# Scan gate and norm moved between the steps of the output product; the scan's state part scaled in its PSUM bank

## The chip, the cores and the metric

The kernel runs on 1 core of one Trainium2 chip. The metric is the device time of one execution in microseconds (us). Names of engines as in the profile: PE is TensorE (PEld its weight loads), DVE is VectorE, ACT is ScalarE, POOL is GpSimd, SP is the engine that issues most DMAs (SPq is its queue of instructions). Loops count from 0.

## The reference

The program is two layers of one hybrid block (attention, convolution, recurrence, Fourier mix), and then one layer of a second block: latent attention, a state-space scan over 10 chunks of 128 positions with 16 heads in both directions, a gate, a norm, an output product, and a feed-forward part. The change lies in the second block alone:

```python
# y: the scan's output (1024 positions x 1024), both directions and the skip term added up
# z: a gate, silu(projection), computed earlier and stored in HBM
y = y * z
y = y * rsqrt(mean(y * y, axis=-1) + EPS) * ssd_norm_2
mix = concatenate([attention (1024 columns), y (1024 columns)], axis=-1) @ w_out_2   # 2048 x 1024
x = x + gate * rms_norm(mix, mix_post_norm_2)
```

In the scan, the output of a chunk has a state part, `(C S) * exp(a)` (S is the state carried from chunk to chunk, `exp(a)` one factor for each position and head), and a part within the chunk. Everything is float32.

## The kernel before, in words

Each stage is a block with one instruction list per engine and a barrier at its end (`k.done`); nothing of a stage starts before all engines have left the one before. The order within a stage is written out by hand, and semaphores pass results between engines. The three stages in question:

**The scan, `ssd_scan` (L1825).** Ten units u; w is the direction (0 forward, 1 backward), g a group of 8 heads (512 columns). The first two units carry only the state; units 2 to 9 (i = u - 2 is 0 to 7) give output. POOL multiplies the inputs by the factors of their positions (`weigh`, L1908: xw for the state, xd for the part within the chunk), decays the state (`decay`, L1926, L1936) and writes the skip term `xs * skip` as the first value of y (`skip_terms`, L1902, L1904). PE does the state part (`off`, L1954), the state's increment (`inc`, L1961) and, per unit, eight products within the chunk (`diag`, L1997). DVE multiplies the state part by `exp(a)` out of PSUM into an SBUF tile `tmp` (L2041) and adds `tmp` to y (`add`, L2053, both operands in SBUF), adds the increment to the state (`state`, L2061), masks the exponentials (`mask`, L2072), and adds the part within the chunk from PSUM to y (`diag`, also L2053). Three PSUM banks are shared in turn by `off` and `inc`: `wait_bank` (L1882) makes a product wait for the one three turns earlier to be used.

**The gate and norm, `normalize` (L579, called at L3738).** For each of 8 tiles of 128 positions: DVE multiplies y by z (L704), ACT squares and sums (L729), DVE and ACT form the root and its reciprocal (L672, L732, L676), DVE scales (L718), PE transposes 8 blocks (L774), ACT and DVE move four of them each into `ssd_t`, multiplied by the gain (L739, L684). SP loads the z tiles (L802), the 4 MB of attention output (L805) and, after the last z, the first three weight chunks (L126).

**The output product, `project_normalize` (L2550, called at L3742).** Tiles in groups of 3, 3 and 2; each group takes 16 steps kk over 2048 rows of weights: kk 0 to 7 read the attention output, kk 8 to 15 `ssd_t`. In a step ACT rounds the input and one row block of weights (L2869, L2873), DVE forms what the rounding left (L2773, L2776), and PE does 3 products for each tile and half (L2903 to L2905). Rounded tiles are two or three deep, so ACT runs up to two steps ahead of PE. At kk 1 to 7 of groups 1 and 2 the same engines also do the residual, norm and transposes of the group before (`norms`). Before its second step DVE combines some rows that POOL and SP have loaded (`constants`, L2684). Weights come in chunks of 2 MB for 4 steps, in a ring of 3.

The weights' ring lies where the scan keeps its tiles, so the first chunk can't be loaded before the scan is over.

## Time and profile before

| | before |
|---|---|
| median of 3 runs | 4858.21 us (4854.99 to 4859.52) |
| the profiled execution | 4853.79 us, its span 4851.9 us |
| PE, DVE, ACT, POOL busy | 85%, 58%, 44%, 21% of the span |
| the scan, 3563 to 3779 us | 216 us, granted PE clock 0.90 |
| gate and norm, 3779 to 3834 us | 55 us, granted PE clock 0.50 |
| output product, 3834 to 4057 us | 223 us, granted PE clock 0.94 |

Rows of the timeline have the start in the span, the time from the first start to the last end of the instructions merged in them, engine, line, operation, tiles, and how many. In brackets stands how long the engine was idle before, and what ended that. The granted clock is a share of the full one: 0.50 is the lower of its two levels (1.2 GHz), 1.00 the upper (2.4 GHz).

### The profile page before, as it was taken

What the parts mean: (1) busy time and instruction counts of PE and PEld (TensorE: products, weight loads), DVE (VectorE), ACT (ScalarE), POOL (GpSimd) and SP (SyncE); (2) the same over time, 40 slices, a digit from 0 to 9 for tenths busy, and PEclk for the clock granted to TensorE, in tenths of its full rate; (3) what the DMA queues carried; (4) which work ended last, traced back from release to release, by engine and by line L of the source; (5) the groups of instructions that cost most, each with busy time, mean ns of one, the idle gap of its engine ahead of it and who ended that gap; (6) DMA issues with size and microseconds to landing.
All of it is one profiled execution on the core that took longest, in us unless ns stands there. A gap on an engine that the chain in (4) does not pass through costs nothing. (4 is left out here: it accounts for less than half of the span.)

```text
span 4851.9 us, 58640 instructions
## 1 busy us (share of the span) xinstructions
PE 4126.1 (85%) x21892; PEld 3166.3 (65%) x21892; DVE 2830.4 (58%) x4301; ACT 2151.2 (44%) x3807; POOL 1011.2 (21%) x1178
## 2 busy tenths in 40 slices
PE   5989798977989887976779999979949687999898
PEld 4765576766765666655547667657736576888676
DVE  3745566966655557965434544535967555565545
ACT  4532245424532346324446666644524344444334
POOL 0001002510001001500047777720046000110100
PEclk7989899988999998988989999989969798999999
DMA  5100012554100011032000000022000434111233
GB/s 161 35 14 1 32 44 97 211 183 161 38 18 1 32 35 61 2 99 86 19 12 8 5 5 5 1 87 62 10 2 1 178 130 118 35 53 52 74 139 135
DMA packets 178077, 295.81 MB, mean 61 GB/s; under 512 B 43322, under 2 KB 105914, under 8 KB 177796
## 3 DMA queue, kind: packets, MB, share of 16 engines
q1 hardware_dynamic: 177044, 291.83, 17.8%
q8 instruction: 177, 2.90, 0.3%
q14 instruction: 104, 0.85, 0.1%
q0 software_dynamic: 608, 0.08, 0.0%
q10 hardware_dynamic: 144, 0.15, 0.0%
HBM read 261.53 MB, written 30.51 MB: 60 GB/s over the span
## 5 line engine op out<-in xcount | busy, mean ns | idle before, releaser
L497 DVE TENSOR_TENSOR x_low<-buf_a,x_high 128x1280 fp32r<-128x1280 f32 (+5 forms) x368 | 373.8, 1016 | 441.4 <-ACT x_high L466 438.3
L523 PE MATMUL ps<-x_high,w_high 128*128 128x512 f32 (+1 forms) x1344 | 497.4, 370 | 106.1 <-DVE w_low L501 101.5
L466 ACT CAST x_high<-buf_a 128x1280 fp32r<-128x1280 f32 (+5 forms) x368 | 324.8, 882 | 570.5 <-PE ps L525 490.5
L524 PE MATMUL ps<-x_low,w_high 128*128 128x512 f32 (+1 forms) x1344 | 485.4, 361 | 0.0
L525 PE MATMUL ps<-x_high,w_low 128*128 128x512 f32 (+1 forms) x1344 | 484.4, 360 | 0.0
L2903 PE MATMUL ps<-w_high,x_high 128*128 128x512 f32 x896 | 369.4, 412 | 109.7 <-DVE w_low L2776 64.6
L3185 POOL TENSOR_TENSOR probs_low<-kr_t,probs_high 128x512 fp32r<-128x512 f32 x320 | 411.2, 1285 | 181.4 <-ACT probs_high L3318 123.1
L3342 DVE TENSOR_REDUCE mx<-ps 128x1 f32<-128x1280 f32 x128 | 191.0, 1492 | 327.8 <-PE ps L3213 327.2
L523 PEld LDWEIGHTS ps<-x_high,w_high 128*128 128x128 f32 x1344 | 259.7, 193 | 178.1 <-DVE x_low L497 116.9
L2904 PE MATMUL ps<-w_low,x_high 128*128 128x512 f32 x896 | 362.6, 405 | 0.0
L2905 PE MATMUL ps<-w_high,x_low 128*128 128x512 f32 x896 | 361.5, 404 | 0.0
L2776 DVE TENSOR_TENSOR w_low<-w,w_high 128x1024 fp32r<-128x1024 f32 x170 | 208.2, 1224 | 256.9 <-ACT w_high L2873 256.8
L2873 ACT CAST w_high<-w 128x1024 fp32r<-128x1024 f32 x170 | 178.2, 1049 | 339.4 <-PE ps L2905 339.4
L2204 PE MATMUL ps<-x_high,w_high 128*128 128x512 f32 x704 | 278.4, 395 | 13.0 <-DVE w_low L2300 13.0
L525 PEld LDWEIGHTS ps<-x_high,w_low 128*128 128x128 f32 x1344 | 259.1, 193 | 38.5
L2903 PEld LDWEIGHTS ps<-w_high,x_high 128*128 128x128 f32 x896 | 177.0, 197 | 161.9 <-issue 124.6
L524 PEld LDWEIGHTS ps<-x_low,w_high 128*128 128x128 f32 x1344 | 260.0, 193 | 32.6
L2206 PE MATMUL ps<-x_high,w_low 128*128 128x512 f32 x704 | 279.8, 397 | 0.0
L2205 PE MATMUL ps<-x_low,w_high 128*128 128x512 f32 x704 | 278.9, 396 | 0.0
L523 PE MATMUL ps<-w_high,x_high 128*128 128x512 f32 (+2 forms) x608 | 219.0, 360 | 61.0 <-DVE w_low L501 57.4
L2296 DVE TENSOR_TENSOR x_low<-attn_t,x_high 128x512 fp32r<-128x512 f32 x176 | 145.6, 828 | 203.6 <-ACT x_high L2249 193.4
L3314 ACT ACTIVATE kr_t<-ps 128x512 f32<-128x512 f32 x320 | 191.6, 599 | 135.2 <-PE ps L3244 74.8
(418 smaller groups left out, 9512.0 us busy)
## 6 DMA issues: line engine op xcount, KB each, us to landing
w<-in_w_out SPq DMA_DIRECT2D x26, 2048.0 KB, 8.2
w<-in_w_mod SPq DMA_DIRECT2D x24, 2048.0 KB, 9.0
w<-in_w_down SPq DMA_DIRECT2D x15, 2048.0 KB, 8.2
w<-in_w_in SPq DMA_DIRECT2D x26, 1024.0 KB, 5.5
w<-in_w_up SPq DMA_DIRECT2D x22, 1024.0 KB, 7.6
w<-in_w_in SPq DMA_DIRECT2D x7, 2048.0 KB, 8.7
x<-in_x SPq DMA_DIRECT2D x16, 512.0 KB, 4.5
scratch_x<-x SPq DMA_DIRECT2D x16, 512.0 KB, 5.2
```

The lines of the kernel that those rows point to most:

```text
L466: act.copy(xh[i % NX][:, 0:s["tn"]], x_of(s)).then_inc(x_high, 1)
L497: dve.tensor_tensor(xl[i % NX][:, 0:s["tn"]], x_of(s), xh[i % NX][:, 0:s["tn"]].bitcast(F32), ALU.subtract).then_inc(x_low, 1)
L523: pe.matmul(g["out"], lhs[0][:, :], rhs[0][:, :], start=(s["kk"] == 0), stop=False)
L524: pe.matmul(g["out"], lhs[0][:, :], rhs[1][:, :], start=False, stop=False)
L525: mm = pe.matmul(g["out"], lhs[1][:, :], rhs[0][:, :], start=False, stop=s["last"])
L2204: pe.matmul(o, wh[w % NW][:, c], xh[x % NX][:, :], start=(kk == 0), stop=False)
L2205: pe.matmul(o, wh[w % NW][:, c], xl[x % NX][:, :], start=False, stop=False)
L2206: mm = pe.matmul(o, wl[w % NW][:, c], xh[x % NX][:, :], start=False, stop=(kk == KD - 1))
L2903: pe.matmul(o, a[:, t], wh[i % NW][:, c], start=(s["kk"] == 0), stop=False)
L2904: pe.matmul(o, a[:, t], wl[i % NW][:, c], start=False, stop=False)
L2905: mm = pe.matmul(o, b[:, t], wh[i % NW][:, c], start=False, stop=s["last"])
L3185: pool.tensor_tensor(prl[g % NPR][:, :], pt[g % NPT], prh[g % NPR][:, :].bitcast(F32), ALU.subtract).then_inc(probs_low, 1)
```

## The change

**In the scan.** `off` on DVE writes its product back into the PSUM bank it read, and `add` takes it from there; `tmp` is gone. The bank is therefore free only after the addition: `wait_bank` waits for `off_added`. POOL issues the skip terms of two chunks after `decay(u)` and ahead of `weigh(u + 1)`, for u = 1 to 4; before it was after `weigh(u + 1)`, for u = 0 to 3.

**Between scan and product.** The `normalize` call is gone. A class `StateNorm` gives ACT, DVE and PE lists of work by step of the product, and `project_normalize` issues one item of each after every step. Tiles 0 to 2 are done in steps 0 to 7 of group 0, tiles 3 to 5 in its steps 8 to 15, tiles 6 and 7 in steps 8 and following of group 1. y is gated and scaled in place; afterwards its rows hold the product's own scratch tiles. The z tiles have three buffers, so the load of tile n, from n = 3 on, waits on SP until tile n - 3 is squared. Each list yields once per step. The attention output comes in three pieces, by group.

```diff
@@ wait_bank
-                pe.wait_ge(off_used, nth(u - CT_, w, g) + 1)
+                pe.wait_ge(off_added, off_at[u, w, g])
@@ POOL
                 decay(u)
+                if 1 <= u < 5:
+                    skip_terms(u - 1)
+                    skip_terms(NLT - u)
                 if u + 1 < U:
                     weigh(u + 1)
-                if u < 4:
-                    skip_terms(u)
-                    skip_terms(NLT - 1 - u)
@@ DVE, off
-                b = tmp[g]
+                o = ps[:, bank_of("off", u, w, g), :]
                 dve.wait_ge(off_ready, nth(i, w, g) + 1)
-                dve.tensor_tensor(heads(b[:, :]), heads(ps[:, bank_of("off", u, w, g), :]), per_head(eac, CT_ + t, g, w), ALU.mult
-                                  ).then_inc(off_used, 1)
-                dve.wait_ge(off_used, nth(i, w, g) + 1)
-                add(t, g, b[:, :])
+                dve.tensor_tensor(heads(o), heads(o), per_head(eac, CT_ + t, g, w), ALU.mult).then_inc(off_scaled, 1)
+                dve.wait_ge(off_scaled, nth(i, w, g) + 1)
+                add(t, g, o)
@@ new class
+class StateNorm(Beside):
+    WINDOWS = {0: (0, 1, 2), KD: (3, 4, 5), 3 * KD: (6, 7)}
+    GATE, SQUARE, MEAN, SCALE, TURN, OUT = (0, 0, 1), (1, 1, 2), (2, 2, 3), (3, 3, 4), (3, 4, 5), (5, 6, 7)
...
+    def load(self, sp, weights):
...
+        attn(0)
+        weights(1)
+        for n in range(3):
+            z(n)
+        sp.dma_start(self.gcol[:, :], self.gain.rearrange("(k p) -> p k", p=P)).then_inc(self.gain_in, 16)
+        weights(3)
+        attn(1)
+        attn(2)
+        for n in range(3, 8):
+            z(n)
...
+    def dve(self, dve):
...
+            for n in ga:
+                dve.wait_ge(self.z_in[n % 3], 16 * (n // 3 + 1))
+                dve.tensor_tensor(self.y[:, n, :], self.y[:, n, :], self.z[n % 3][:, :], ALU.mult).then_inc(self.gated, 1)
...
+    def pe(self, pe, banks_free):
+        for tu in self.parts(self.TURN):
+            for n in tu:
+                banks_free(pe)
+                if n >= 1:
+                    self.wait_banks(pe)
+                pe.wait_ge(self.scaled, n + 1)
...
@@ project_normalize, DVE (ACT and PE alike)
+            parts = beside.dve(dve) if beside else iter(())
             for i, s in enumerate(steps):
...
                 norms(s["kk"], before[s["g"]])
+                next(parts, None)
@@ project_normalize, SP
+            if beside:
+                beside.load(sp, lambda m: ws.load_until(sp, first_chunk + m - W_SLOTS))
+                ws.load_until(sp, first_chunk + 3)
             def load(n):
+                if beside and n < NS:
+                    sp.wait_ge(beside.transposed, 2 * (NS + n + 1))
@@ second_block
-    normalize(k, [dict(t=t, stream=0, src=d["z"][(t - CT_) * P:(t - CT_ + 1) * P, :], res=True, yt=t - CT_, store=None)
-                  for t in range(CT_, NT)], ssdT, None, d["ssd_norm_2"][0], lay, y=y, gates=None,
-              moves=[(attnT[:, :, :], d["attn"].rearrange("(c p) t -> p c t", p=P))])
...
+                      post=d["mix_post_norm_2"][0], beside=StateNorm(k, y, ssdT, d["ssd_norm_2"][0], attnT, rooms))
```

The order on POOL at the scan's start, where xw, xd are weighed inputs, s the states and ssd_y the skip terms. Before:

```order
L1914 TENSOR_TENSOR xw_453_34884<-xs_32719,w_end_34751 128x512 x2
L1914 TENSOR_TENSOR xw_455_34886<-xs_32719,w_end_34751 128x512 x2
L1904 TENSOR_TENSOR ssd_y_34882<-xs_32719,skip_34750 128x512 x4
L1936 TENSOR_TENSOR s_456_34887<-s_457_34888,tot_34752 128x512 x2
L1936 TENSOR_TENSOR s_458_34889<-s_459_34890,tot_34752 128x512 x2
L1914 TENSOR_TENSOR xw_452_34883<-xs_32719,w_end_34751 128x512 x2
L1914 TENSOR_TENSOR xw_454_34885<-xs_32719,w_end_34751 128x512 x2
```

and in the changed kernel, at the same place:

```order
L1915 TENSOR_TENSOR xw_453_34884<-xs_32719,w_end_34751 128x512 x2
L1915 TENSOR_TENSOR xw_455_34886<-xs_32719,w_end_34751 128x512 x2
L1937 TENSOR_TENSOR s_456_34887<-s_457_34888,tot_34752 128x512 x2
L1937 TENSOR_TENSOR s_458_34889<-s_459_34890,tot_34752 128x512 x2
L1905 TENSOR_TENSOR ssd_y_34882<-xs_32719,skip_34750 128x512 x4
L1915 TENSOR_TENSOR xw_452_34883<-xs_32719,w_end_34751 128x512 x2
L1915 TENSOR_TENSOR xw_454_34885<-xs_32719,w_end_34751 128x512 x2
```

The decay of unit 1 now comes ahead of the first skip terms; the input of unit 2 keeps its place.

The order of DMA issues on SP after the scan, before:

```order
L802 DMA x_479_36777<-scratch_z 128x1024
L802 DMA x_480_36778<-scratch_z 128x1024
L802 DMA x_481_36779<-scratch_z 128x1024
L805 DMA attn_t_22019<-scratch_attn 128x8x1024
```

and in the changed kernel (xn is the place of the row that `constants` reads):

```order
L3071 DMA gate_row_497_36793<-scratch_mod 128x1024
L3074 DMA xn_494_36790<-in_mix_post_norm 128x1024
L2583 DMA attn_t_22019<-scratch_attn 128x8x384
L126 DMA w_3_51<-in_w_out 128x4x1024
L2580 DMA z_477_36775<-scratch_z 128x1024
L2580 DMA z_478_36776<-scratch_z 128x1024
L2580 DMA z_479_36777<-scratch_z 128x1024
L2589 DMA gain_col_36778<-in_ssd_norm 128x8x1
L126 DMA w_4_52<-in_w_out 128x4x1024
L126 DMA w_2_50<-in_w_out 128x4x1024
```

Two broadcast rows and a piece of the attention output now stand ahead of the first weight chunk, and the z tiles behind it.

## Rows read from the trace of the kernel before

**Rows 1.** Windows of scan and norm: us, busy by engine, PEclk, DMA share, GB/s.

```profile
3563.00:3779.00 216.00, 165.50 (x816) 117.38 (x816) 151.70 (x188) 74.84 (x160) 135.04 (x128) 0.90 0.00 1
3779.00:3834.00 55.00, 15.93 (x65) 12.76 (x66) 30.41 (x70) 26.42 (x62) 3.55 (x4) 0.50 0.74 277
```

**Rows 2.** Timeline of DVE, first outputs of the scan.

```profile
3583.42 0.69 DVE L2061 TENSOR_TENSOR s<-ps,s 128x512 f32<-128x512 f32 x1 [0.31 <-POOL s L1936]
3586.28 0.69 DVE L2041 TENSOR_TENSOR tmp<-ps,eac 128x512 f32<-128x512 f32 x1 [2.16 <-PE ps L1954]
3587.00 24.87 DVE L2053 TENSOR_TENSOR ssd_y<-tmp,ssd_y 128x512 f32<-128x512 f32 x1
```

**Rows 3.** Timeline of POOL, the same stretch.

```profile
3579.28 4.04 POOL L1936 TENSOR_TENSOR s<-s,tot 128x512 f32<-128x512 f32 x4
...
3607.28 4.04 POOL L1904 TENSOR_TENSOR ssd_y<-xs,skip 128x512 f32<-128x512 f32 x4
3617.96 1.04 POOL L1936 TENSOR_TENSOR s<-s,tot 128x512 f32<-128x512 f32 x1 [6.64 <-DVE s L2061]
```

**Rows 4.** Timeline of PE, first products within the chunk of i = 0 and 1.

```profile
3612.52 1.97 PE L1997 MATMUL ps<-xd,e 128*128 128x64 f32 x8 [25.42 <-DVE e L2072]
...
3636.36 1.10 PE L1997 MATMUL ps<-xd,e 128*128 128x64 f32 x8 [1.96 <-DVE e L2072]
```

**Rows 5.** Timeline of DVE, first items of later units of the scan.

```profile
3633.58 0.69 DVE L2041 TENSOR_TENSOR tmp<-ps,eac 128x512 f32<-128x512 f32 x1 [2.54 <-PE ps L1954]
3634.30 1.40 DVE L2053 TENSOR_TENSOR ssd_y<-tmp,ssd_y 128x512 f32<-128x512 f32 x1
...
3654.41 0.69 DVE L2041 TENSOR_TENSOR tmp<-ps,eac 128x512 f32<-128x512 f32 x1 [2.54 <-PE ps L1954]
...
3760.90 0.69 DVE L2053 TENSOR_TENSOR ssd_y<-tmp,ssd_y 128x512 f32<-128x512 f32 x1
```

**Rows 6.** Timeline from the scan's end to the product's start.

```profile
3778.35 0.69 DVE L2053 TENSOR_TENSOR ssd_y<-ps,ssd_y 128x512 f32<-128x512 f32 x1 [0.60 <-PE ps L1997]
3780.06 1.28 SPq L802 DMA_DIRECT2D x<-scratch_z  x3
...
3797.26 1.22 DVE L704 TENSOR_TENSOR x<-ssd_y,x 128x1024 f32<-128x1024 f32 x1
...
3802.36 1.22 DVE L704 TENSOR_TENSOR x<-ssd_y,x 128x1024 f32<-128x1024 f32 x1
...
3831.38 1.04 ACT L2873 CAST w_high<-w 128x1024 fp32r<-128x1024 f32 x1
...
3833.82 0.77 PE L2903 MATMUL ps<-w_high,x_high 128*128 128x512 f32 x1 [5.13 <-DVE w_low L2776]
```

**Rows 7.** Windows of 4 us: attention load, then broadcasts with x tiles.

```profile
3788.00:3792.00 4.00, 0.00 (x0) 0.00 (x0) 1.39 (x4) 2.63 (x4) 0.00 (x0) 0.50 1.02 416
...
3836.00:3840.00 4.00, 4.00 (x16) 3.21 (x15) 0.00 (x0) 0.12 (x1) 0.00 (x0) 0.84 1.03 243
```

**Rows 8.** DMA issues by line, 3775 to 3850, then 3846 to 4070.

```profile
w<-in_w_out SPq DMA_DIRECT2D x3, 2048.0 KB, 13.2
...
w<-in_w_out SPq DMA_DIRECT2D x9, 2048.0 KB, 7.9
```

**Rows 9.** Timeline of the product: step length on DVE; transposes on PE; start of group 2.

```profile
3959.87 1.23 DVE L2776 TENSOR_TENSOR w_low<-w,w_high 128x1024 fp32r<-128x1024 f32 x1 [2.38 <-ACT w_high L2873]
...
3963.95 1.23 DVE L2776 TENSOR_TENSOR w_low<-w,w_high 128x1024 fp32r<-128x1024 f32 x1 [2.38 <-ACT w_high L2873]
...
3932.20 1.03 PE L2887 MATMUL ps<-ident,xn 128*128 128x128 f32 x8
3932.99 0.48 PE L2903 MATMUL ps<-w_high,x_high 128*128 128x512 f32 x1
...
3844.65 0.47 PE L2903 MATMUL ps<-w_high,x_high 128*128 128x512 f32 x1 [0.79 <-DVE w_low L2776]
...
3985.41 0.77 PE L2903 MATMUL ps<-w_high,x_high 128*128 128x512 f32 x1 [6.32 <-DVE tmp L2702]
```

More of the change, by code:

```diff
@@ L1886, in wait_bank @@
             if kind == "off":
-                pe.wait_ge(off_used, nth(u - CT_, w, g) + 1)
+                pe.wait_ge(off_added, off_at[u, w, g])
             else:
                 pe.wait_ge(state_out, nth(u, w, g) + 1)
+    off_at = {(u, w, g): nth(u - CT_, w, g) + 1 for u in range(CT_, U) for w in range(2) for g in range(2)}
     def diag_bank(g):
@@ L2555, in project_normalize @@
+def project_normalize(k, y, kt, tiles, sizes, xt, mod_cols, gain, lay, gates, post=None, pre=None, stored=None, beside=None):
     nc, ps, d, ws = k.nc, k.ps, k.d, k.ws
@@ L2587, in project_normalize @@
     wh, wl = ([lay(f"w_{p}{i}", [P, D], F32R) for i in range(NW)] for p in ("high", "low"))
-    xs = [lay(f"x{i}", [P, D]) for i in range(NS)]
-    tmp = [lay(f"tmp{i}", [P, D]) for i in range(NB)]
+    places = beside.places if beside else {}
+    xs = places["x"] if beside else [lay(f"x{i}", [P, D]) for i in range(NS)]
+    tmp = places["tmp"] if beside else [lay(f"tmp{i}", [P, D]) for i in range(NB)]
     xn = [lay(f"xn{i}", [P, D]) for i in range(2)] if xt is not None else []
-    trash = lay("trash", [P, D])
+    trash = places["trash"] if beside else lay("trash", [P, D])
     stat = lay("stat", [P, 3, 3, nt])
@@ L2594, in project_normalize @@
     gate_row = {s: lay(f"gate_row{s}", [P, D]) for s in sorted({w["stream"] for w in with_y})}
-    post_row = lay("post_row", [P, D]) if post is not None else None
+    post_row = (xn[0] if beside else lay("post_row", [P, D])) if post is not None else None
     pre_row = lay("pre_row", [P, D]) if pre is not None else None
@@ L2598, in project_normalize @@
     gcol = lay("gain_col", [P, KD])
+    first_chunk = ws.taken - len(groups) * n_chunks
     sems = k.sems("rows_in", "cols_in", "squared", "rooted", "dve_chain", "scaled", "transposed", "evac_act", "evac_dve",
@@ L2794, in square_root @@
                     act.wait_ge(squared, sq_index[n, kind] - 1)
+                elif beside:
+                    act.wait_ge(beside.squared, 6)
                 act.activation(trash[:, :], data, ACT.Square, accum_out=st[:, 0:1]).then_inc(squared, 1)
@@ L2864, in norms @@
                     tile_of(transposes_out, mine, 2)
+            parts = beside.act(act) if beside else iter(())
             for i, s in enumerate(steps):
@@ L2868, in _ @@
                     act.wait_ge(ws.products, steps[i - NX]["after"])
+                if beside:
+                    beside.ready(act, s["g"], s["kk"])
                 act.copy(xh[i % NX][:, 0:s["tn"]], y(s["kk"], s["t0"], s["tn"])).then_inc(x_high, 1)
@@ L2874, in _ @@
                 norms(s["kk"], before[s["g"]])
+                next(parts, None)
             for kk in range(1, 8):
@@ L2879, in _, with banks_free @@
         def _(pe):
+            turned = [0]
+            def banks_free(engine):
+                if turned[0]:
+                    engine.wait_ge(evac_act, turned[0])
+                    engine.wait_ge(evac_dve, turned[0])
+            parts = beside.pe(pe, banks_free) if beside else iter(())
             def transposes(n):
                 pe.wait_ge(scaled, n + 1)
+                turned[0] = n + 1
+                if beside:
+                    beside.wait_banks(pe)
                 for half in range(2):
@@ L2911, in _ @@
                     tile_of(transposes, before[s["g"]], turn_at.index(s["kk"]))
+                next(parts, None)
             if xt is not None:
@@ L2950, in _ @@
                     sp.wait_ge(stored[i], 16 * n_store[i])
-    k.done(sems)
+    k.done(sems + (beside.sems if beside else []))
 class Gates(Beside):
```

102 lines of the change are left out of this document (92 added, 10 removed).

## The prediction

> **What bounds the kernel now.** I read the page first for the whole, then the windows over the second block, then the timelines of one engine after another around each place that the change touches. The whole is PE's: 85% busy. The change lies in three neighbouring stages, and each has another limit.
>
> In the scan PE sets the pace once it runs. A unit takes 20.83 us, from one state part on DVE to the next (3633.58 to 3654.41) [rows 5]. The first unit with output is the exception. DVE's first addition of `tmp` to y starts at 3587.00 and is on record for 24.87 us, where the same operation takes 0.69 us later on [rows 2, 5]. It ends at 3611.87. POOL ran without a gap until 3607.28 + 4.04 = 3611.32 and then waited for DVE [rows 3]. PE stood for 25.42 us, waiting for the mask behind that addition [rows 4]. So one addition held up the three engines. I take the cause to be its two SBUF inputs: the state addition at 3583.42, with one input in PSUM, took 0.69 us while POOL was inside its run of decays that began at 3579.28 [rows 2, 3]. In later units the first such addition takes 1.40 us, and with POOL done with its work, at 3760.90, 0.69 us [rows 5].
>
> The Trainium skill says the same in "SBUF — State Buffer", section "Who interferes with whom": a DVE instruction with two SBUF inputs contends with a GpSimd instruction that reads SBUF, and the pair of ports is an exclusive lock for one whole instruction. By that rule the addition would wait for one POOL instruction, some 1 us; the trace has 24.87 us, so here back-to-back POOL instructions kept it out. By the page alone the change would win about 1 us at this place instead of the 23.1 us below.
>
> Between scan and product PE has 64 transposes in 55 us at a granted clock of 0.50 [rows 1]. The scan's last addition ends at 3779.04, the product's first matmul starts at 3833.82: 54.8 us [rows 6]. Each tile takes 5.10 us there, a chain over DVE, ACT, DVE and PE (3797.26 to 3802.36) [rows 6].
>
> In the product PE sets the pace: a step of three tiles is 4.08 us, and DVE sits idle 2.38 us of it ahead of its weights' part, waiting for ACT, which waits for PE [rows 9].
>
> **The change, part by part.** All sums are against the profiled execution (4853.79 us, its span 4851.9 us). It lies 4.4 us below the median of the runs, so I add the difference to the median at the end.
>
> *1. The long addition.* Its second input is in PSUM now, so it shows no wait for POOL: 0.69 us as at 3583.42. What comes late next is POOL's own work. POOL took 1.01 us for each instruction, four in 4.04 us. The decay of unit 1 started at 3579.28 behind four skip terms [rows 3]; now it starts where those did, at about 3575.3, and is done at 3579.3, and the skip terms of chunks 0 and 7 are done by 3583.3. Unit 2's xw keeps 3583.28 to 3587.28, and the first two xd, which PE's first product within the chunk needs, are done at 3589.28 (two more instructions). DVE's state part, scaling, addition and masks start 4 us earlier than before and are ready by about 3585, so POOL is the last. Before, that product started at 3612.52 [rows 4]; now at 3589.4. Gain 23.1 us. The rest of unit i = 0 I leave as it was: 3636.36 - 3612.52 = 23.84 us [rows 4], 3 us longer than 20.83, from a slow start after PE's idle time. PE will be idle again ahead of it, for about 6 us. POOL's further instructions (decay, skip, xw, xd, 16 of them, 16.2 us) fit into a unit.
>
> *2. The addition in units 1 to 6.* The masks stand behind it on DVE, and PE waits 1.96 us for them [rows 4]. 1.40 becomes 0.69 us, six times: gain 6 x 0.71 = 4.3 us. The later part of a unit is PE's own.
>
> *3. The banks.* The wait for the addition instead of the scaling holds a bank 0.7 us longer. The product three turns on comes at least 2 us later in PE's order: nothing. DVE writing PSUM instead of SBUF isn't in the trace; the nearest rows, reading PSUM, have 0.69 against 0.69 us [rows 2, 5]. I take 0; if it were 0.1 us more for each of 32, with a quarter of them ahead of PE, 1 us.
>
> *4. From the scan's end to the first product.* The first DMA still goes out at 3780.06, 1.0 us after the scan [rows 6]. Ahead of the first weights in the queue stand two broadcast rows (1.0 MB written), 1.6 MB of attention output, then 2.1 MB of weights. Loads of this queue land in its order: three chunks issued at one time landed at 13.2 us in the median, one alone at 7.9 us [rows 8], so a second chunk costs 5.3 us. Large loads ran at 416 GB/s (0.416 MB in a us), the stretch with broadcasts at 243 GB/s [rows 7]. Broadcasts 1.05 / 0.243 = 4.3 us, attention 1.57 / 0.416 = 3.8 us, or, its pieces being 1.5 KB, up to 4.8 us; I take 4.3. A chunk then lands 7.9 us later, its latency in it. Sum: 3780.9 + 4.3 + 4.3 + 7.9 = 3797.4. From the rounding of the weights to the first matmul it is 3833.82 - 3831.38 = 2.4 us [rows 6]. First matmul at 3799.8: 20.8 us after the scan, where it was 54.8. Gain 34.0 us. With all at 416 GB/s it would be 36; with the attention piece and the weights at 243 GB/s too, 28.
>
> *5. The first steps.* PE loses 0.79 us before its third step, because DVE waits for rows that POOL loads [rows 9]. These loads now have the 20 us before the first matmul. Gain 0.8 us.
>
> *6. What the norm costs inside the product.* PE gets 64 transposes: 8 x 0.8 us at the full clock (3932.20 to 3932.99) [rows 9], and perhaps 0.2 us of wait behind each eight. Cost 8 x 0.9 = 7.2 us. DVE's heaviest step has two gates (2 x 1.22 us [rows 6]) beside its own 1.8 us: 4.2 us against 4.08, with a lead of up to two steps, so hidden. ACT's has two squares, below that. Each transpose set waits for the banks of the one before to be emptied, one step later on DVE and ACT; they get to it about 3.7 us after PE has begun the step, and PE needs 5 us for step and transposes: hidden, with about 1 us to spare.
>
> *7. The fourth chunk.* On SP it stands behind the z loads, the last of which waits for the square of tile 4 in step 9. That happens when PE ends step 7, about 3837; with two squares it is 3840.5. Behind the two z tiles (2 x 1.3 us) the chunk lands at about 3840.5 + 1 + 2.6 + 7.9 = 3852; the rounding for step 12 should start by 3852.5. Near the edge: I take 0.5 us, and up to 5 if the queue is slower.
>
> Sum: -23.1 - 4.3 - 34.0 - 0.8 + 7.2 + 0.5 = -54.5 us. On the profiled execution 4799.3; on the median 4803.7. The changes of group (6.32 us of PE idle [rows 9]) and the last group's norm stay.
>
> **The rivals.**
> *A. The long wait moves.* If what holds DVE is not the second SBUF input but any addition into y while POOL runs without a gap, parts 1 and 2 go. For: the state additions that ran beside POOL wrote another tile. Against: the additions of 0.69 us from PSUM to y, and the 24.87 us ends with POOL's run and nothing else. 4858.2 - 27.1 = 4831.
> *B. The queue.* The fourth chunk, a z tile or the first weights come late, 5 us at one, or twice: 3 loads more between others than before. For: SP is one instruction list, and a wait in it holds every later load. Against: rates of [rows 7]. 4809 to 4816.
> *C. More is won.* Without the slow start of unit 0 (3 us) and with the first weights at the better rate (2 us): 4798.
> *D. The other side.* The norm's chain doesn't hide: PE reaches each set of transposes before `scaled` and waits the chain of 5.10 us [rows 6] for each of 8 tiles, 40.8 us, and the clock falls to 0.50 after such waits, as where the product restarted after 6.32 us [rows 9]; with 2 us for each of 8 restarts that is 56.8 us. It turns the result from about 54 us on: 4804 + 57 = 4861. Against: gate, square, mean and scale are each issued one step before they are needed, 4 us for at most 2.5 us of work.
> *E. The change does nothing for the gap*, because the attention output and weights set its length anyway: 5.7 MB and latency. Against: three quarters of that load is now behind the first matmul. It would leave -27 + 7 = -20: 4838.
>
> **How the numbers follow.** The forecast, 4796 to 4810, has 0.62; B 0.15; C 0.12; A 0.06; E 0.02; D 0.02; 0.01 for no difference. What this kernel's measurement can tell from none is 0.2%, 10 us, either way. A, B, C, E and the forecast all lie below 4848: faster 0.97, same 0.01, slower 0.02. The range takes in B and C and their bounds: 4791 to 4820.
>
> **What would show it.** In the scan: no addition into y above 1 us, PE's first product within the chunk near 3589, units of 20.1 us, the scan ending near 3752. Then 20 us, not 55, to the first matmul, which waits for weights, with the lower clock at its start. In the product: 8 transpose sets of about 0.8 to 1 us each, DVE without a wait for POOL's rows, and PE's idle time in step 12 near zero. The prediction is wrong if an addition of PSUM and y waits for POOL, if the first matmul comes later than 28 us after the scan, or if PE waits at the transposes for `scaled`.

## The result, and the profile after

| | before | after |
|---|---|---|
| median of 4 runs each, us | 4857.15 (4854.99 to 4859.52) | 4801.23 (4798.93 to 4803.31) |
| ratio, with its 95% interval | | 0.9885 (0.9868 to 0.9902) |
| profiled execution, us; its span | 4853.79; 4851.9 | 4798.93; 4797.1 |

The change takes 55.9 us off, 1.15%. The forecast was 4803.7 us with a range of 4791 to 4820. In the profiled executions the difference is 54.9 us, where the sum of the terms said 54.5. It comes from these stages, each read between the same two instructions of the two traces:

| stage | from, to | before | after |
|---|---|---|---|
| scan | POOL's first `xw`, end of DVE's last addition into y | 215.99 | 186.71 |
| gap | to the product's first matmul | 54.78 | 20.55 |
| product | to PE's first transposes behind its last wait for DVE | 215.37 | 224.38 |
| tail | to the next stage's first matmul | 19.25 | 19.31 |
| the rest | to the end of the span | 783.46 | 783.53 |

The work ahead of the scan took 0.4 us less by chance (POOL's first `xw` at 3563.05 and at 3562.62); in the kernels below that item starts anywhere from 3560.0 to 3566.0. So single traces are compared by their stages here, not by the time of day in them.

Windows of the scan and of the gap after the change, which answer to [rows 1]; the columns are the same (us, busy time of PE, PEld, DVE, ACT and POOL, PEclk, DMA share, GB/s):

```profile
3562.60:3749.33 186.73, 161.81 (x816) 114.62 (x816) 120.96 (x188) 74.84 (x160) 129.13 (x128) 0.95 0.00 1
3749.33:3769.87 20.54, 0.00 (x0) 0.03 (x1) 1.93 (x4) 2.91 (x4) 2.69 (x3) 0.55 0.90 300
```

DVE's busy time in the scan falls from 151.70 to 120.96 us with the same 188 instructions: most of what went was never work, but waiting that is on record as busy (the long addition alone is 24.2 of these 30.7 us). The mean granted clock rises from 0.90 to 0.95.

DVE's first outputs, against [rows 2], and its first items of two later units, against [rows 5]:

```profile
3580.21 0.70 DVE L2042 TENSOR_TENSOR ps<-ps,eac 128x512 f32<-128x512 f32 x1 [0.51 <-PE ps L1955]
3580.95 0.69 DVE L2053 TENSOR_TENSOR ssd_y<-ps,ssd_y 128x512 f32<-128x512 f32 x1
...
3609.67 0.70 DVE L2042 TENSOR_TENSOR ps<-ps,eac 128x512 f32<-128x512 f32 x1 [2.54 <-PE ps L1955]
3610.40 0.69 DVE L2053 TENSOR_TENSOR ssd_y<-ps,ssd_y 128x512 f32<-128x512 f32 x1
...
3629.79 0.70 DVE L2042 TENSOR_TENSOR ps<-ps,eac 128x512 f32<-128x512 f32 x1 [2.55 <-PE ps L1955]
```

The addition of 24.87 us takes 0.69 us now, and so does each later one. Scaling in the PSUM bank takes 0.70 us where writing `tmp` took 0.69. A unit takes 20.12 us (3609.67 to 3629.79).

PE's first products within the chunk, against [rows 4]:

```profile
3589.06 1.94 PE L1998 MATMUL ps<-xd,e 128*128 128x64 f32 x8 [8.03 <-POOL xd L1924]
...
3611.74 1.10 PE L1998 MATMUL ps<-xd,e 128*128 128x64 f32 x8 [1.25 <-DVE e L2072]
```

In the first, PE waits for POOL's `xd` and no longer for DVE's mask; in the second the wait behind DVE's addition is 1.25 us instead of 1.96.

The gap, against [rows 6] and [rows 8]: the queue and ACT, then the loads between 3749 and 3775 with the median time from issue to landing.

```profile
3750.35 0.33 SPq L3071 DMA_DIRECT2D gate_row<-scratch_mod  x1
3750.73 0.43 SPq L3074 DMA_DIRECT2D xn<-in_mix_post_norm  x1
3751.20 0.43 SPq L2583 DMA_DIRECT2D attn_t<-scratch_attn  x1
3751.68 0.58 SPq L126 DMA_DIRECT2D w<-in_w_out  x1
```

```profile
3762.31 0.51 ACT L3008 CAST x_high<-attn_t 128x384 fp32r<-128x384 f32 x1 [15.58 <-DMA attn_t<-scratch_attn]
...
3767.43 1.04 ACT L3012 CAST w_high<-w 128x1024 fp32r<-128x1024 f32 x1 [4.61 <-DMA w<-in_w_out]
```

```profile
gate_row<-scratch_mod SPq DMA_DIRECT2D x1, 512.0 KB, 4.6
xn<-in_mix_post_norm SPq DMA_DIRECT2D x1, 512.0 KB, 5.6
```

The two rows have landed at about 3755.0 and 3756.3, the attention piece by 3762.3, the first weights by 3767.4, each behind the one before. The product's first matmul follows at 3769.88, 2.45 us after its weights are there.

The product, against [rows 9]:

```profile
3789.13 1.03 PE L2673 MATMUL ps<-ident,ssd_y 128*128 128x128 f32 x8
3789.92 0.48 PE L3055 MATMUL ps<-w_high,x_high 128*128 128x512 f32 x1
...
3794.21 1.03 PE L2673 MATMUL ps<-ident,ssd_y 128*128 128x128 f32 x8
```

A set of eight transposes holds PE for 0.79 us (3789.13 to 3789.92), and none of the eight sets shows a wait for `scaled` or for a bank.

### The profile page after: what moved, and what is told of

It reads as the page before. It is cut to its first block and busy times, and to the rows that moved or that the text cites. A ratio compares the mean times of both kernels' runs of the same rounds, so it can differ in the third digit from the quotient of the medians.

```text
span 4797.1 us, 58620 instructions
## 1 busy us (share of the span) xinstructions
PE 4119.3 (86%) x21892; PEld 3159.2 (66%) x21892; DVE 2796.7 (58%) x4299; ACT 2147.5 (45%) x3807; POOL 1006.1 (21%) x1177
## 3 DMA queue, kind: packets, MB, share of 16 engines
q1 hardware_dynamic: 180164, 291.84, 18.1%
```

## The experiments

Twelve kernels were run. Their medians stand against runs of the kernel before on the same chip. "Scan", "gap" and "product" are the stages of the table above, read from each kernel's own trace.

| kernel | median | against before | ratio (95%) | scan | gap | product |
|---|---|---|---|---|---|---|
| e_psum | 4824.48 | -30.7 | 0.9940 (0.9925 to 0.9954) | 185.79 | 55.39 | |
| e_order | 4851.56 | -3.6 | 0.9993 (0.9983 to 1.0002) | 212.15 | 54.81 | |
| e_norm | 4827.20 | -28.0 | 0.9945 (0.9930 to 0.9960) | 216.06 | 20.68 | 223.52 |
| e_pause | 4832.26 | -22.9 | 0.9954 (0.9940 to 0.9969) | 195.32 | 55.06 | |
| e_early | 4835.47 | -20.0 | 0.9957 (0.9942 to 0.9972) | 195.99 | 54.60 | |
| e_first | 4833.08 | -22.4 | 0.9956 (0.9941 to 0.9971) | 195.43 | 54.76 | |
| e_rows | 4800.45 | -54.5 | 0.9886 (0.9872 to 0.9901) | 186.60 | 17.23 | 224.20 |
| e_xd | 4796.69 | -58.3 | 0.9880 (0.9865 to 0.9894) | 182.49 | 20.52 | 224.61 |
| e_align | 4797.27 | -57.7 | 0.9883 (0.9866 to 0.9899) | 186.58 | 20.55 | 222.10 |
| e_turn16 | 4808.37 | -46.6 | 0.9902 (0.9887 to 0.9917) | 186.53 | 20.53 | 231.72 |
| e_best | 4792.45 | -63.0 | 0.9871 (0.9855 to 0.9888) | 183.45 | 17.71 | 221.08 |
| e_best2 | 4790.30 | -65.2 | 0.9869 (0.9853 to 0.9886) | 184.12 | 17.27 | 220.91 |

### The parts one by one: e_psum, e_order, e_norm

e_psum is the kernel before with the state part scaled in its bank:

```
-                b = tmp[g]
+                o = ps[:, bank_of("off", u, w, g), :]
...
-                dve.tensor_tensor(heads(b[:, :]), heads(ps[:, bank_of(...), :]), per_head(...), ALU.mult)
+                dve.tensor_tensor(heads(o), heads(o), per_head(...), ALU.mult)
...
-                add(t, g, b[:, :])
+                add(t, g, o)
... in wait_bank:
-                pe.wait_ge(off_used, nth(u - CT_, w, g) + 1)
+                pe.wait_ge(off_added, off_at[u, w, g])
```

Expected: 

> The kernel before, with the state part scaled in its PSUM bank and nothing else; POOL keeps its old order and the norm stays a stage of its own. My theory (the second SBUF input lets POOL's back-to-back instructions keep DVE out): the first addition into y takes 0.7 us instead of 24.87, PE's first product within the chunk starts at about 3589 to 3590, later units take 20.1 us: 26 to 28 us less than before, about 4830. Rival A (any addition into y waits for POOL): no change, the long addition stays. A second rival, that the reordering of POOL is needed for the gain: less than 20 us.

Measured: 30.7 us less than before; the scan 30.2 us shorter, where 26 to 28 were expected (the rest is the unit behind the first product, 21.77 us for 23.84, and the slow unit of point 2 below). DVE's and PE's timelines:

```profile
3586.00 0.69 DVE L2054 TENSOR_TENSOR ssd_y<-ps,ssd_y 128x512 f32<-128x512 f32 x1
```

```profile
3588.58 1.07 PE L1999 MATMUL ps<-xd,e 128*128 128x64 f32 x8 [2.50 <-POOL xd L1925]
3610.35 1.11 PE L1999 MATMUL ps<-xd,e 128*128 128x64 f32 x8 [1.25 <-DVE e L2073]
```

POOL, in its old order, had no gap here either (from 3562.16 on), and DVE's addition took 0.69 us inside that run. So the operand in PSUM alone removes the long wait, and rival A falls. The new order of POOL isn't needed; with the operand in PSUM the scan is 0.9 us longer with it (186.71 against 185.79, from one profile of each). PE's product starts 26.42 us after POOL's first item here and 26.44 after the change. But DVE's scaling, addition and masks come later in the old order, so PE stands idle for 2.50 us instead of 8.03 ahead of that product, and the product itself takes 1.07 us instead of 1.94.

e_order moves POOL's skip terms and changes nothing else:

```
                 decay(u)
+                if 1 <= u < 5:
+                    skip_terms(u - 1)
+                    skip_terms(NLT - u)
                 if u + 1 < U:
                     weigh(u + 1)
-                if u < 4:
-                    skip_terms(u)
-                    skip_terms(NLT - 1 - u)
```

Expected: 

> The kernel before, with POOL's skip terms moved ahead of the next unit's weighing and nothing else; the addition keeps tmp in SBUF. My theory: the addition starts some 4 us earlier and still waits until POOL's run ends, which now comes about 4 us earlier because the skip terms of chunks 2 and 5 are behind the decay that waits: an addition of 24 to 26 us, PE's first product within the chunk at about 3608, later units still 20.8 us; 4 to 5 us less than before, about 4853. Rival (the order of POOL is what ended the long wait): 23 us less.

Measured: 3.6 us less, within this measurement's noise; the scan 3.8 us shorter. The addition in DVE's timeline:

```profile
3584.30 26.53 DVE L2053 TENSOR_TENSOR ssd_y<-tmp,ssd_y 128x512 f32<-128x512 f32 x1
```

It is still there, ends at 3610.83, and POOL's run ended at 3610.28 (its last four `xd` are 3606.24 + 4.04). Before the change it ended 0.55 us behind POOL too (3611.87 and 3611.32 [rows 2, 3]). The order of POOL's work alone doesn't end the wait, so the rival falls.

e_norm has the scan of before, with `tmp` and the old order of POOL, and the norm between the steps of the product:

```
-    normalize(k, [...], ssdT, None, d["ssd_norm_2"][0], lay, y=y, gates=None, moves=[...])
-    project_normalize(..., post=d["mix_post_norm_2"][0])
+    project_normalize(..., post=d["mix_post_norm_2"][0],
+                      beside=StateNorm(k, y, ssdT, d["ssd_norm_2"][0], attnT, rooms))
```

Expected: 

> The scan as before (tmp in SBUF, old order of POOL), the norm tile by tile between the steps of the product as in the changed kernel. My theory: the parts add up. The gap from scan to product falls from 54.8 to 20.6 us, the product takes 9 us longer, as in the changed kernel: 25 us less than before, about 4832. Rival (the gap's gain hangs on the faster scan, or the product's loss does): off by more than 5 us from that.

Measured: 28.0 us less by the medians. Counted from POOL's first item, the profiled execution is 23.8 us shorter: scan +0.1, gap -34.1, product +8.2, and 2.1 us more than in the kernel before in what comes behind the product, which the edit doesn't touch. The theory's 25 lies between the two figures. The gap and the product repeat those of the changed kernel within 1 us, so the parts add up. e_psum's scan and this gap make 64.3 us, and with the product's 9 to pay about 55.

### What kept DVE waiting: e_pause, e_early, e_first

These three are the kernel before with one wait added on POOL, each in another place; `tmp` stays in SBUF.

```
e_pause, in the unit loop of POOL:
+                if u == 1:
+                    pool.wait_ge(off_added, 1)
                 if u < 4:
                     skip_terms(u)
e_early, in weigh(u):
+                if u == 2:
+                    pool.wait_ge(off_ready, 1)
e_first, in the unit loop of POOL:
+                if u == 0:
+                    pool.wait_ge(inc_ready, nth(1, 1, 0) + 1)
                 if u < 4:
                     skip_terms(u)
```

Expected of e_pause: 

> The kernel before, with one wait on POOL: after the first unit's xd and before the skip terms of chunks 1 and 6 it waits until the first addition into y is done. My theory (back-to-back POOL instructions keep the addition out, and it gets in when POOL stops): the addition starts near 3587.0 and ends within 1 us of POOL's stop near 3591.3, so 4 to 5 us long instead of 24.87; PE's first product within the chunk near 3593, 18 to 20 us less than before, about 4838. Rival (the addition waits for something else than POOL's run, its tile y or a semaphore): it stays near 25 us and the time doesn't change, or grows by the 4 us that POOL lost.

Measured: 22.9 us less. DVE and POOL:

```profile
3585.20 5.02 DVE L2055 TENSOR_TENSOR ssd_y<-tmp,ssd_y 128x512 f32<-128x512 f32 x1
...
3592.06 0.84 DVE L2055 TENSOR_TENSOR ssd_y<-tmp,ssd_y 128x512 f32<-128x512 f32 x1
```

```profile
3585.64 4.04 POOL L1923 TENSOR_TENSOR xd<-xs,dt 128x512 f32<-128x512 f32 x4
3590.31 4.49 POOL L1904 TENSOR_TENSOR ssd_y<-xs,skip 128x512 f32<-128x512 f32 x4 [0.63 <-DVE ssd_y L2055]
```

POOL stops at 3589.68, the addition ends at 3590.22: once more 0.54 us behind. So it was POOL's run that held it; its tile and its semaphores were ready all along. But the next rows speak against my wording of the cause. From 3590.31 POOL runs without a gap for over 50 us. The additions that meet this run, early or late in it, wait at most 0.8 us (0.84 us long at 3592.06, 1.45 at most), while the first four POOL instructions take 4.49 us instead of 4.04. So it isn't the length of the run either. "POOL back to back keeps DVE out" is too wide: it is true here only of the first run. The next two kernels ask what differs in it.

Expected of e_early: 

> The kernel before, with one wait on POOL in another place: ahead of the first unit's xw it waits until PE has made the first state part, so POOL idles from 3583.3 to about 3586.2 and then runs without a gap again. DVE's first addition into y starts some 0.8 us into that run, not within the idle time. What is open: in the kernel with a pause inside the long addition, later additions that met a gapless run of POOL waited at most 0.4 us, each to about the end of one POOL instruction, while the first one was held for the whole run. Theory 1 (a run of POOL that has once been interrupted lets DVE in at the next instruction's end): the addition takes at most 1.7 us, PE's first product within the chunk near 3592, 18 to 21 us less than before. Theory 2 (DVE's first addition of two SBUF inputs is held until POOL stops, whatever POOL did before): it lasts until the run ends near 3614, the time grows by about 3 us over before.

Measured: 20.0 us less. DVE and POOL:

```profile
3587.48 0.91 DVE L2055 TENSOR_TENSOR ssd_y<-tmp,ssd_y 128x512 f32<-128x512 f32 x1
```

```profile
3586.80 5.01 POOL L1916 TENSOR_TENSOR xw<-xs,w_end 128x512 f32<-128x512 f32 x4 [2.79 <-PE ps L1956]
3591.78 4.04 POOL L1925 TENSOR_TENSOR xd<-xs,dt 128x512 f32<-128x512 f32 x4
```

Expected of e_first: 

> The kernel before, with one wait on POOL still earlier: ahead of its first skip terms (3575.3) it waits for PE's next to last state product of unit 1, an idle time of under 1 us; then it runs without a gap, and DVE's first addition into y meets it some 11 us into that run. With the idle time 3.3 us ahead of the addition (the run before this one) the addition took 0.91 us. Theory 1 (one interruption of POOL since the start of the stage is enough): the addition takes at most 1.7 us, 19 to 22 us less than before. Theory 2 (only a recent interruption lets DVE in; a long run shuts it out again): the addition lasts until the run ends near 3612, the time is within 1 us of before.

Measured: 22.4 us less. DVE and POOL:

```profile
3588.12 1.07 DVE L2055 TENSOR_TENSOR ssd_y<-tmp,ssd_y 128x512 f32<-128x512 f32 x1
```

```profile
3575.60 4.04 POOL L1904 TENSOR_TENSOR ssd_y<-xs,skip 128x512 f32<-128x512 f32 x4 [1.26 <-PE ps L1963]
3579.60 4.04 POOL L1936 TENSOR_TENSOR s<-s,tot 128x512 f32<-128x512 f32 x4
3583.60 4.04 POOL L1914 TENSOR_TENSOR xw<-xs,w_end 128x512 f32<-128x512 f32 x4
3587.60 5.01 POOL L1923 TENSOR_TENSOR xd<-xs,dt 128x512 f32<-128x512 f32 x4
```

Theory 1 holds in both. One idle time of POOL of 1.26 us, 12.5 us ahead of the addition, with no DVE instruction of two SBUF inputs in between, takes the wait from 24 us to 0.4. POOL's group gets longer instead, 5.01 for 4.04 us. The kinds of POOL's instructions are the same in all four kernels, and its run was gap-free at the addition in each. What differs is only whether POOL has paused since it began the stage. A wait that is met at once isn't enough: in the kernel before, POOL's decays and `xw` between 3595 and 3603 wait for semaphores and lose no time by it, and the addition stays held. Nor does the idle time ahead of the stage count, 365 us in the kernel before. Why a run that never paused since then holds DVE to its end isn't settled by these runs, and all of them look at one place of one kernel.

### The sizes of the other terms: e_rows, e_xd, e_align, e_turn16

All four are the changed kernel with one edit.

```
e_rows, in StateNorm.load (the two broadcasts are a function now, called here and not first):
         attn(0)
         weights(1)
         for n in range(3):
             z(n)
+        rows()
...
```

Expected: 

> The changed kernel, with the loads of the two broadcast rows (gate and post norm) issued behind the first attention piece, the first chunk of weights and the first three z tiles instead of ahead of them all. My theory for the gap's length (the loads of this queue land in its order, and what stands ahead of the first weights sets the first matmul): the first weights land about 4.3 us earlier, the first matmul comes 16 to 17 us after the scan's end instead of 20.55, and the rows, needed by DVE after step 1, come early enough: 4 us less than the changed kernel, 57 to 61 us less than before. Rival (the weights' own transfer and latency set it, the rows are small): gap within 1 us of 20.55. A second rival: DVE waits for the rows or z between steps 1 and 2, and PE gets the 4 us back as idle time in step 2.

Measured: the gap is 17.23 us, 3.3 less, and nothing is given back in the product (224.20 against 224.38). ACT and DVE:

```profile
3765.66 1.04 ACT L3013 CAST w_high<-w 128x1024 fp32r<-128x1024 f32 x1 [4.73 <-DMA w<-in_w_out]
```

```profile
3772.64 1.23 DVE L2826 TENSOR_TENSOR gate_row<-gate_row,xn 128x1024 f32<-128x1024 f32 x1 [0.73 <-DMA xn<-in_mix_post_norm]
```

The weights are there 14.8 us behind the scan's end (3750.88) instead of 18.1, and DVE waits 0.73 us for the row, which PE doesn't feel. The queue's order sets the gap; the two rows cost 3.3 us of it, for which I had 4.3. The medians don't show it (-54.5 against -55.9 in another comparison): 3 us is below what they tell.

```
e_xd, in POOL's unit loop:
+                if u == 1:
+                    skip_terms(0)
+                    weigh_d(2)      # the xd part of weigh, now apart
+                    weigh(2)
+                    skip_terms(NLT - 1)
+                    continue
...
```

Expected: 

> The changed kernel, with POOL's order changed in one unit: after the decay of unit 1 the skip terms of chunk 0, then the first unit's xd, its xw, and the skip terms of chunk 7 last. In the changed kernel PE waits 8.03 us for xd at its first product within the chunk, with the masks ready 6 us earlier. My theory (POOL is what comes last there): the first product starts about 6 us earlier, the next one that needs xw about 5 us earlier, with less idle time the clock falls less: 4 to 6 us less than the changed kernel. Rival (masks or xw hold PE by then): less than 2 us.

Measured: the scan is 4.2 us shorter, the least that the theory gave. PE:

```profile
3582.59 1.15 PE L2007 MATMUL ps<-xd,e 128*128 128x64 f32 x8 [2.01 <-POOL xd L1926]
3586.50 2.08 PE L1971 MATMUL ps<-xw,btm 128*128 128x512 f32 x2 [1.80 <-POOL xw L1915]
...
3607.10 1.10 PE L2007 MATMUL ps<-xd,e 128*128 128x64 f32 x8 [1.25 <-DVE e L2081]
```

The first product comes 6.0 us sooner after POOL's first item (20.42 for 26.44), the unit then takes 24.51 us for 22.68, with PE waiting twice for POOL. That POOL was last ahead of this first product is shown. Of the 6.0 us, 1.8 are lost again in the unit behind it, whose granted clock is 0.86 where it was 0.88.

e_align pads two small tiles, so that the buffers 0 and 1 of `x_high` (the rounded inputs, PE's stationary tiles) start at a multiple of 512 bytes and not 128 bytes past one. Addresses are counted from the start of the kernel's own stretch of SBUF, as the kernel lays them out. Buffer 2 and all of `x_low` start at a multiple in both. Besides, the gate's row and three small tiles behind `x_high` move, which PE doesn't read.

```
-        self.gcol = lay("gain_col", [P, KD])
-        self.stat = lay("stat", [P, 3, LAT // P])
+        self.gcol = lay("gain_col", [P, P])
+        self.stat = lay("stat", [P, 3, P // 3])
...
```

Expected: 

> The changed kernel, with the two small tiles that stand ahead of x_high in the same stretch of SBUF (gain_col and stat of the norm) made 512 bytes long each, so that the buffers 0 and 1 of x_high start at a multiple of 512 bytes and no longer 128 bytes past one; nothing else moves or changes. In the changed kernel the product's matmuls follow each other at 0.2333 us in two steps of three and at 0.2267 in the third, by the buffer of x_high that a step uses (before: 0.2267 in all). My theory (the start address of buffers 0 and 1 costs it): 0.2267 in all steps, 3 us less in the product, 3 us less in all. Rival (the place, the busier DVE or the DMA costs it, not the address): no change, 0.2333 stays.

Measured: the product takes 222.10 us, 2.3 less. PE in the changed kernel, in a step with buffer 2 and in one with buffer 0 (the second row of a pair starts 14 matmuls after the first):

```profile
3781.28 0.39 PE L3057 MATMUL ps<-w_high,x_low 128*128 128x512 f32 x1
...
3784.46 0.39 PE L3056 MATMUL ps<-w_low,x_high 128*128 128x512 f32 x1
...
3785.40 0.39 PE L3057 MATMUL ps<-w_high,x_low 128*128 128x512 f32 x1
...
3788.66 0.40 PE L3056 MATMUL ps<-w_low,x_high 128*128 128x512 f32 x1
```

3.18 us for 14 is 0.227 each, 3.26 is 0.233. In e_align the same place in the step of buffer 0:

```profile
3787.03 0.39 PE L3055 MATMUL ps<-w_high,x_high 128*128 128x512 f32 x1
...
3790.21 0.39 PE L3057 MATMUL ps<-w_high,x_low 128*128 128x512 f32 x1
```

3.18 us again. Over the whole product the mean distance of two matmuls without a wait is 0.2275 us before the change, 0.2317 after it, 0.2315 in e_norm and 0.2279 in e_align. So the start address of two small buffers accounts for nearly all of it, while DVE, ACT and the DMA have the same work as after the change. In the steps of buffers 0 and 1 every third matmul reads `x_low`, whose address is a multiple of 512 bytes, and the distance to the next one is the same behind all three kinds, 0.233 to 0.234 us. So the shift slows the whole step and not only the matmuls that read the shifted tile; why isn't shown. Of the 3 us that the theory gave, 0.8 came back as a wait that had been hidden. ACT gets the fourth chunk of weights late in both kernels, by 3.51 us after the change (the first row below) and by 4.25 here, and with PE faster it shows (the second row, of e_align):

```profile
3823.56 1.05 ACT L3012 CAST w_high<-w 128x1024 fp32r<-128x1024 f32 x1 [3.51 <-DMA w<-in_w_out]
```

```profile
3827.62 0.47 PE L3055 MATMUL ps<-w_high,x_high 128*128 128x512 f32 x1 [0.77 <-DVE w_low L2909]
```

In the changed kernel PE felt at most 0.16 us of its wait (the next matmul comes 0.95 us behind the start of the transposes at 3825.07, where it is 0.79 behind the other sets).

e_turn16 does each of the norm's transposes twice:

```
-                    for q in range(4):
+                    for q in (0, 0, 1, 1, 2, 2, 3, 3):
```

Expected: 

> The changed kernel, with each of the norm's 64 transposes inside the product done twice in a row. My theory (PE sets the pace of these steps and a set of eight costs its own time on PE and nothing beside it): 8 x 0.79 = 6.3 us more than the changed kernel. Rival 1 (the transposes stand in idle time of PE): below 2 us more. Rival 2 (the chain of norm, transposes and emptying of the banks is near its limit, 1 us to spare by my estimate): the emptying comes late and PE waits, over 9 us more.

Measured: the product is 7.3 us longer, 0.92 for each further eight. PE:

```profile
3792.25 1.91 PE L2673 MATMUL ps<-ident,ssd_y 128*128 128x128 f32 x16
3793.92 0.47 PE L3055 MATMUL ps<-w_high,x_high 128*128 128x512 f32 x1
```

Sixteen hold PE for 1.67 us where eight hold it for 0.79, and nothing behind them waits. That is 0.88 for each further eight, a little more than the 0.79 of the theory. They stand in PE's own time, so rival 1 falls. The chain behind them has slack even at twice the load, so rival 2 falls.

### Together: e_best and e_best2

e_best takes the edits of e_rows and e_align, and e_xd's with halves: skip terms of chunk 0, two `xd`, `xw` forward, two `xd`, `xw` backward, skip terms of chunk 7. e_best2 has whole parts as e_xd, and the skip terms of chunk 7 behind the decay of unit 2.

```
e_best, against e_xd (with the edits of e_rows and e_align beside):
                 if u == 1:
                     skip_terms(0)
-                    weigh_d(2)
-                    weigh(2)
+                    for h in range(2):
+                        weigh_d(2, (h,))
+                        weigh(2, (h,))
                     skip_terms(NLT - 1)
                     continue
e_best2, against e_xd (with the same two beside):
                     weigh(2)
-                    skip_terms(NLT - 1)
                     continue
+                if u == 2:
+                    skip_terms(NLT - 1)
```

Expected of e_best: 

> The changed kernel with three edits together: the broadcast rows behind the first weights and z tiles, the buffers of x_high on 512 bytes, and the first unit's POOL work in the order skip terms of chunk 0, half of xd, xw forward, other half of xd, xw backward, skip terms of chunk 7. If the single gains add up (stage by stage in the traces: gap 3.3, product 2.3, scan 4.2 us) and the halved order brings PE's first product with xw another 2 us forward: 11 to 12 us less than the changed kernel, about 67 less than before. Rival (with the rows later and the scan shorter, the queue or DVE's constants become the wait, or the shorter steps run into the weights' rounding): 7 us or less.

Expected of e_best2: 

> The changed kernel with the rows behind the first weights and z tiles, the buffers of x_high on 512 bytes, and POOL's order in the first unit as in the run that moved xd ahead of xw, with the skip terms of chunk 7 now behind the decay of unit 2. In the combination before this one the halved order made the scan 183.45 us, the plain one alone 182.49, and in both DVE waits 5.5 us for the decay of unit 2 at its first state product. If that decay is what comes last there: scan 181 us, gap 17.5, product 221: 12 us less than the changed kernel, 1.5 to 3 us less than the combination before this one. Rival (PE's own work sets that unit): scan 182.5 us, 1 us less than the combination before.

Measured: counted from POOL's first item, both profiled executions are 10.4 us shorter than the changed kernel's (1224.04 and 1224.10 against 1234.48). By the medians e_best2 is 65.2 us under before, 0.9869 (0.9853 to 0.9886), where the change has 0.9885 (0.9868 to 0.9902). By the stages it beats the changed kernel too; by the medians that isn't shown, since the two intervals overlap. Both are short of the 11 to 12 us that were expected. The gaps (17.71, 17.27) and the products (221.08, 220.91) came as expected, the scan did not: 183.45 and 184.12 us, where e_xd alone has 182.49. With the finer orders of POOL it was longer, in the one profile that each kernel has. Windows of e_xd and of e_best2, equally far behind POOL's first item (26 to 32 us); columns as above:

```profile
3588.17:3590.17 2.00, 2.00 (x10) 1.80 (x9) 0.00 (x0) 0.00 (x0) 2.00 (x3) 0.50 0.00 0
3590.17:3592.17 2.00, 2.00 (x12) 1.44 (x12) 0.62 (x2) 1.33 (x3) 2.00 (x3) 0.97 0.00 0
3592.17:3594.17 2.00, 2.00 (x12) 1.43 (x12) 1.75 (x4) 1.01 (x3) 2.00 (x3) 1.00 0.00 0
```

```profile
3586.00:3588.00 2.00, 2.00 (x10) 1.79 (x9) 0.61 (x1) 0.00 (x0) 2.00 (x3) 0.50 0.00 0
3588.00:3590.00 2.00, 2.00 (x5) 1.25 (x5) 0.44 (x2) 0.99 (x3) 2.00 (x3) 0.50 0.00 0
3590.00:3592.00 2.00, 2.00 (x10) 1.52 (x9) 1.02 (x2) 0.37 (x1) 2.00 (x3) 0.58 0.00 0
```

PE is busy in all of them; in e_best2 the granted clock stays at 0.50 (1.2 GHz) some 3.5 us longer. The decay that I took for the last comer was 2 us earlier (DVE waits 3.62 us for it and no longer 5.50), and PE computed at half speed instead. In e_best the clock was back at 1.00 by then; DVE still waited 5.62 us for the decay, PE 1.63 us for the mask behind it, and the clock fell to 0.50 once more. The best scan of all is e_xd's, so its order with the other two edits should give about 1223 us by these stages, an estimate; that one wasn't run.

## Why the prediction was right, point by point

*The whole.* Forecast -54.5 us on the profiled execution, measured -54.9. The mechanism was right in each part that carried the sum; no rival came about. That the sum fits within 0.4 us is luck in part: the scan gave 1.9 us more than its two terms, and the product cost 2.1 us more than its three, and these nearly cancel. (The upper bound of rival B is added up wrongly: 5 us twice make 4814 and not 4816. Nothing hangs on it.)

*1. The long addition.* PE's first product within the chunk was to come 23.1 us sooner; it came 23.0 sooner after POOL's first item (26.44 us, where before had 3612.52 - 3563.05 = 49.47), and POOL's `xd` was the last comer, as forecast. PE stood idle 8.03 us ahead of it, where I had about 6. In two things the number was right and the reason wasn't. I gave the two SBUF inputs and POOL's back-to-back instructions as the cause. The first half is shown by e_psum. The second is true of a POOL run without any pause since the stage began, and of no other that these runs show (e_pause, e_early, e_first). And the working of the term leaned on the new order of POOL, which e_psum shows to be worth nothing there: in the old order the product starts at the same place.

The Trainium skill's "SBUF — State Buffer", section "Who interferes with whom", has the pair of ports locked for one whole instruction. I had set it aside for this place. The runs agree with it everywhere but there: additions that meet POOL after a pause take at most 1.56 us, and the four POOL instructions that the first of them meets 4.49 to 5.01 instead of 4.04, so each side waits for at most one instruction of the other. What no sentence of that section covers is the 24.87 us in the run that had not paused.

*Unit 0, kept at 23.84 us.* From PE's first product of this unit to that of the next it took 22.68. Of the 1.16 us gained, 0.71 is the first of the six shares of the next point, since that addition lies between the two products; the other 0.45 is new.

*2. The addition in the units.* Six times 0.71 us, as forecast; a unit went from 20.83 to 20.12 us. Beyond that, one unit of the kernel before took 22.46 us, which I had not seen. It begins at 3696.80; its window and that of the unit ahead of it:

```profile
3696.80:3719.26 22.46, 20.27 (x101) 14.88 (x100) 15.04 (x22) 9.36 (x20) 13.04 (x13) 0.92 0.00 1
3675.97:3696.80 20.83, 18.64 (x101) 13.62 (x100) 15.05 (x22) 9.35 (x20) 13.03 (x13) 1.00 0.00 1
```

The same instructions at a granted clock of 0.92 for 1.00. It is no chance of one execution: each of the six kernels with `tmp` has one such unit in its profile (22.46 to 22.53 us, the third to the sixth of the seven steps from unit to unit), and none of the eight with the product in its bank has. That makes 1.6 us. The scan gave 29.3 us where terms 1 and 2 had 27.4; this unit (1.6) and unit 0 (0.45) are the difference.

*3. Banks and writing PSUM.* 0.70 for 0.69 us, PE waits for no bank: 0, as taken.

*4. The gap.* 20.8 forecast, 20.55 measured. The parts differ more than the sum: the two rows cost 3.3 us (e_rows) where I had 4.3, so the attention piece and the weights took more than their terms. The sum also begins at 3780.9, where its own first DMA goes out at 3780.06; from there it gives 19.9 us.

*5. The first steps.* DVE's constants no longer wait for POOL's loads: -0.8, as forecast.

*6. The transposes, and what the sum left out.* I had 7.2 us for them, 0.2 us of wait behind each eight in it. There was no such wait. The first matmul behind each eight takes 0.08 us longer to the next, so they make 8 x 0.87 = 7.0, and e_turn16 puts them at 8 x 0.92 = 7.3. But the product got 9.0 us longer, not 6.9 (7.2 + 0.5 - 0.8). Most of the rest is a thing that I had not looked for: the change puts small tiles ahead of `x_high`, and the new addresses cost 2.3 us or, without the wait that this uncovered, 3.1 (e_align). I read the diff's instructions and not its layout.

*7. The fourth chunk.* It was late: ACT waited 3.51 us for it. PE lost at most 0.2 us by it, where I had 0.5; e_align shows that there was nothing to spare: there PE waits 0.77 us.

## What to carry to other kernels

- Look for DVE instructions with two SBUF inputs whose recorded time is far above that of the same form elsewhere. Putting one input into PSUM removed 24 us here; one short pause of POOL, earlier in the same stage, removed all but 0.2 to 0.4 us of the same wait, and cost one line.
- When loads share a queue, sort them by when they are needed: 1 MB of broadcast rows ahead of the first weights cost 3.3 us of pure wait, and 0.7 us hidden when they stood behind.
- A diff moves addresses as well as instructions. If PE's spacing differs by some per cent in two steps of three, look at the buffers that rotate.

## What the runs showed that I had not expected

- In this scan, POOL's first run, as long as it hasn't paused, holds a DVE instruction of two SBUF inputs until it ends (24.87, 26.53 us; in e_pause 5.02), and the instruction ends 0.54 to 0.55 us behind it. After one pause of POOL (0.63, 1.26 or 2.79 us) the same meeting costs DVE at most 0.9 us.
- Matmuls of 512 columns follow each other at 0.227 us in steps whose `x_high` starts at a multiple of 512 bytes (counted as in e_align) and at 0.233 in steps where it starts 128 bytes past one. Other shifts weren't tried.
- Getting PE's inputs ready earlier does not help by itself, if the last of them comes at the same time: after the change PE idled 8.03 us ahead of its first product and the product took 1.94 us, in e_psum 2.50 us ahead of it and it took 1.07. The granted clock in the first unit was 0.88 and 0.92. In e_best and e_best2 too, an earlier input came with a lower clock for some us.
